# Expert rows weighted, gated and added straight into the residual's rows by the scatter, in a Trainium2 encoder layer

## The reference

```python
x = x + gt1 * token_mixer(h1)                     # attention half, not touched by the change
h = rms_norm(x, g_ffn) * (1.0 + sc2) + sh2
x = x + gt2 * hier_moe(h)                         # top-1 group, top-2 of its 8 experts
return rms_norm(x, g_final)

# hier_moe: 32 experts, each (silu(h @ w_gate) * (h @ w_up)) @ w_down, 1024 -> 512 -> 1024
# rows of a token's two experts are weighted by topw (k = 0, 1) and summed
out = jnp.einsum('nk,nkd->nd', topw, picked)
```

## Time and profile before

| what | value |
|---|---|
| median of three executions | 3067.68 us |
| the profiled execution | 3061.92 us |
| its span, first to last instruction | 3059.7 us |
| busy: PE, DVE, ACT, POOL | 2762.8, 1735.5, 1502.2, 817.3 us |
| mean granted TensorE clock | 0.954 |
| moved by DMA | 451.19 MB |
| router's last VectorE operations, about | 2014 to 2017 us |
| first and last `gate_up` start | 2031.47 and 2929.20 us |
| last scatter lands | 2968 us |

### The profile page before, as it was taken

How to read it: one execution, slowest core, us unless ns; L and a number is a source line. 1 busy time by engine, 2 the same in 40 slices (tenths; PEclk the granted TensorE clock), 3 DMA queues, 4 the chain that set the end, 5 groups by cost and what they waited for, 6 DMA issues and landing times.

```text
span 3059.7 us, 49933 instructions
## 1 busy us (share of the span) xinstructions
PE 2762.8 (90%) x14228; PEld 2320.1 (76%) x14229; DVE 1735.5 (57%) x3141; ACT 1502.2 (49%) x2615; POOL 817.3 (27%) x617
## 2 busy tenths in 40 slices
PE   8899999999999996899999799759999999999960
PEld 2399999999888875788888588647777787877740
DVE  3555655566667666545441244476765635375859
ACT  2455666667544443444432222246655634375744
POOL 1244444554322112244434111101111111111110
PEclk9999999999999998899999899869999999999985
DMA  7500000000000002443433344358976835486978
GB/s 263 202 24 25 27 23 25 25 24 25 22 19 16 10 11 64 133 138 129 138 121 113 137 165 161 128 196 309 345 273 249 302 144 219 140 329 235 366 285 339
DMA packets 195890, 451.19 MB, mean 147 GB/s; under 512 B 39959, under 2 KB 91159, under 8 KB 193773
## 3 DMA queue, kind: packets, MB, share of 16 engines
q1 hardware_dynamic: 176812, 389.46, 36.1%
q0 software_dynamic: 14400, 52.44, 4.5%
q10 hardware_dynamic: 4608, 8.39, 0.7%
HBM read 380.01 MB, written 70.21 MB: 147 GB/s over the span
## 4 chain that ended last, share of the span: by engine, by line
PE 72%; DVE 9%; issue 8%; DMA 6%; ACT 3%; DVEq 1%; POOL 1%; SPq 1%; ACTq 0%; POOLq 0%
PE bank L1672 14%; PE bank L1887 13%; PE bank L1771 5%; PE bank L1815 4%; DMA sb_w_in<-in_w_gate_up 3%; PE S_ps L1898 3%; PE E_ps L1898 3%; PE O_ps L1737 3%; PE S_ps L1771 3%; PE S_ps L1718 3%; PE E_ps L1771 3%; PE S_ps L1720 3%; PE bank L1638 2%; PE E_ps L1704 2%; PE S_ps L1815 1%
## 5 line engine op out<-in xcount | busy, mean ns | idle before, releaser
L1887 PE MATMUL bank<-sb_gu,sb_x_hiT 128*128 (+1 forms) x1568 | 500.5, 401 | 16.7 <-DVE sb_x_loT L1542 16.7
L724 POOL TENSOR_TENSOR sb_h_lo<-sb_hT,sb_h_hi 128x1024 fp32r<-128x1024 f32 x128 | 336.9, 2632 | 611.1 <-ACT sb_h_hi L839 611.1
L1672 PE MATMUL bank<-sb_w_hi,sb_h_hi 128*128 (+1 forms) x1024 | 402.0, 393 | 15.4 <-issue 9.0
L1887 PEld LDWEIGHTS bank<-sb_gu,sb_x_hiT 128*128 128x128 f32 x1568 | 297.7, 192 | 82.5 <-issue 17.7
L1672 PE MATMUL bank<-sb_w_hi,sb_h_lo 128*128 (+1 forms) x1024 | 344.7, 337 | 0.0
L1672 PE MATMUL bank<-sb_w_lo,sb_h_hi 128*128 (+1 forms) x1024 | 343.9, 336 | 0.0
L1528 DVE TENSOR_TENSOR sb_gu<-sb_w_in,sb_gu 128x1024 f32 (+1 forms) x256 | 303.4, 1223 | 60.0 <-ACT sb_gu L1069 55.7
L1069 ACT ACTIVATE sb_gu<-sb_w_in 128x1024 f32 (+1 forms) x256 | 262.8, 1057 | 129.5 <-DMA sb_w_in<-in_w_gate_up 114.8
L1887 PE MATMUL bank<-sb_gu,sb_x_loT 128*128 (+1 forms) x784 | 312.0, 398 | 0.0
L763 POOL TENSOR_TENSOR sb_g_lo<-sb_g_raw,sb_g_hi 128x1408 fp32r<-128x1408 f32 x64 | 212.5, 3341 | 338.1 <-ACT sb_g_hi L944 338.1
L1672 PEld LDWEIGHTS bank<-sb_w_hi,sb_h_hi 128*128 128x128 f32 x1024 | 193.9, 189 | 31.1 <-issue 19.1
(11 more groups left out here) (346 smaller groups left out, 6106.5 us busy)
## 6 DMA issues: line engine op xcount, KB each, us to landing
sb_w_in<-in_w_gate_up SPq DMA_DIRECT2D x256, 512.0 KB, 5.3
sb_w_in<-in_w_expert_down SPq DMA_DIRECT2D x128, 512.0 KB, 5.5
sb_g_raw<-in_w_gb SPq DMA_DIRECT2D x64, 704.0 KB, 4.1
sb_wada<-in_w_ada SPq DMA_DIRECT2D x24, 1024.0 KB, 7.7
sb_yp<-y_d SPq DMA_DIRECT2D x16, 1024.0 KB, 6.7
sb_w_raw<-in_w_qkv SPq DMA_DIRECT2D x128, 96.0 KB, 2.0
sb_x_round<-in_x SPq DMA_DIRECT2D x4, 2048.0 KB, 12.6
mT_d<-sb_mg ACTq DMA_DIRECT2D x32, 256.0 KB, 2.1
```

What stands on the lines that cost most here:

```text
L724: nc.gpsimd.tensor_tensor(h_lo[c][:], tile_src(g, T), h_hi[c][:].bitcast(F32), ALU.subtract).then_inc(sem("h_lo_ready"), 1)
L1672: last = nc.tensor.matmul(bank[c][:, 0:PASS_COLS].rearrange("p (a m) -> p a m", a=1), x[c][:, k, :], w[:, ds(row + k, 1), :], start=(k == ...
L1887: last = nc.tensor.matmul(PS[j][:].rearrange("p (a n) -> p a n", a=1), x[:, k, :], gu[:, ds(gu_row(e, part, k), 1), j * DE:(j + 1) * DE], ...
```

## The change

- The scatter adds (`compute_op=ALU.add`) the finished rows into `x1_d`, at the token's row. `x1_d` has 128 pad rows now, `h2_d` 128 instead of 64. One index table, `row_idx` = max(token, pair - 2048), serves both the gather and the scatter. `y_d` is gone.
- The rows are finished before the scatter: ScalarE's copy out of PSUM takes the pair's weight as its scale (`w_row`, one number per row), and VectorE multiplies by the gate (`gate_rows`), which stands in PSUM banks 6 and 7 (`GT2`). The hidden rows are therefore transposed into bank 2, with two new waits on TensorE.
- The weights of a block come by a new indirect gather (`weights_in`) from `w_d`, into which ScalarE stores `pair_w` once.
- In a block that opens an expert, ScalarE and VectorE convert pieces 0 to 3 (`EARLY`), then do the head of the block, then pieces 4 to 7 (`LATE`), then the tail. TensorE waits for the weights' low parts piece by piece.
- The last stage loads the sums in eight transfers of two tiles, all at once, into buffers of their own, and only squares, scales and stores. It is written out without loops.
- SP sends the gate's row and the pads (four of 256 KB, one of 512 bytes) where it sent three rows and one pad.

```diff
+                for n, (t, row) in enumerate(((gt1b, 2), (A2b, 4), (B2b, 3), (gt2b, 5))):
...
-                sp.dma_start(h2_d[SEQ:SEQ + PAD_ROWS // 2, :], zero_rows[:]).then_inc(sem("pads_out"), 16)
+                for pads in (h2_d, x1_d):
+                    for at in (SEQ, SEQ + PAD_ROWS // 2):
+                        sp.dma_start(pads[at:at + PAD_ROWS // 2, :], zero_rows[:]).then_inc(sem("pads_out"), 16)
+                sp.dma_start(w_d[2 * SEQ:2 * SEQ + PAD_ROWS, :].rearrange("(a n) b -> a (n b)", a=1), zero_rows[0:1, 0:PAD_ROWS]).then_inc(sem("pads_out"), 16)
...
+        sp.wait_ge(sem("experts_done"), 1)
+        for r in range(PAIRS):
+            sp.dma_start(acc[:, 2 * r:2 * r + 2, :], accv[:, 2 * r:2 * r + 2]).then_inc(sem(ACC_IN[r][0]), 16)
+        for t in range(TT):
             sp.wait_ge(sem("out_ready"), t + 1)
+            sp.dma_start(ov[:, t, :], acc[:, t, :]).then_inc(sem("out_stored"), 16)
...
         def scatter_block(g):
+            nc.gpsimd.tensor_copy(si, row_idx[:, ds(g, 1)]).then_inc(sem("si_ready"), 1)
             pool.wait_ge(sem("si_ready"), g + 1)
-            pool.wait_ge(sem("y_ready"), g + 2)
+            pool.wait_ge(sem("y_gated"), g + 1)
...
+            nc.gpsimd.indirect_dma_start(x1_d, bass.IndirectOffsetOnAxis(ap=si, axis=0), y_sb[:], None, compute_op=ALU.add).then_inc(sem("y_out"), 16)
+
+        def weights_in(g):
+
+            nc.gpsimd.tensor_copy(wi, scatter_idx[:, ds(g, 1)]).then_inc(sem("wi_ready"), 1)
+            pool.wait_ge(sem("wi_ready"), g + 1)
+            pool.sem_inc(sem("row_dmas"), 1)
+            nc.gpsimd.indirect_dma_start(w_row[:], None, w_d, bass.IndirectOffsetOnAxis(ap=wi, axis=0)).then_inc(sem("w_in"), 16)
...
         with pool.Fori(1, total) as g:
             pool.wait_ge(sem("xgT_done"), g + 2)
             gather_block(g + 2)
             scatter_block(g - 1)
+            weights_in(g)
             pool.wait_ge(sem("y_out"), 16 * g)
             pool.sem_inc(sem("y_free"), 1)
...
+        act.wait_ge(sem("rows_in"), 80)
+        act.wait_ge(sem("logits_ready"), TT)
+        for j in range(2):
+            last = nc.scalar.activation(GT2[j][:], gt2b[:, j * 512:(j + 1) * 512], ACT.Copy)
+        last.then_inc(sem("gt2_ready"), 1)
...
         def rows_out(g):
             act.wait_ge(sem("down_done"), g + 1)
             act.wait_ge(sem("y_free"), g + 1)
+            act.wait_ge(sem("w_in"), 16 * (g + 1))
             for j in range(2):
+                last = nc.scalar.activation(y_sb[:, j * 512:(j + 1) * 512], PS[4 + j][:], ACT.Copy, scale=w_row[:, 0:1])
...
+                    next_expert_high(g, e, EARLY)
+                    block_head(g)
+                    next_expert_high(g, e, LATE)
+                    block_tail(g)
                     down_high(g, e)
...
+        for r in range(PAIRS):
+            squares_of(2 * r)
+            squares_of(2 * r + 1)
+            if r > 0:
+                roots(r - 1)
+        roots(PAIRS - 1)
...
-        link(nc.vector.tensor_scalar(gather_idx[:], scatter_idx[:], 1, None, ALU.logical_shift_right))
+        link(nc.vector.tensor_scalar(token_i[:], scatter_idx[:], 1, None, ALU.logical_shift_right))
+        link(nc.vector.scalar_tensor_tensor(row_idx[:], scatter_idx[:], -float(SEQ), token_i[:], ALU.add, ALU.max))
...
+        def gate_rows(g):
+            dve.wait_ge(sem("y_ready"), g + 2)
+            for j in range(2):
+                cols = slice(j * 512, (j + 1) * 512)
+                last = nc.vector.tensor_tensor(y_sb[:, cols], y_sb[:, cols], GT2[j][:], ALU.mult)
+            last.then_inc(sem("y_gated"), 1)
+
+        def block_tail(g):
+            if not isinstance(g, int):
+                gate_rows(g - 1)
             dve.wait_ge(sem("hT_high"), g + 1)
...
+        def finish(r):
+            dve.wait_ge(sem("rms"), ROUNDS + TT + r + 1)
+            nc.vector.reciprocal(rstd3[:, 2 * r:2 * r + 2], rms3[:, 2 * r:2 * r + 2]).then_inc(sem("rstd"), 1)
+            dve.wait_ge(sem("rstd"), ROUNDS + TT + r + 1)
+            for t in (2 * r, 2 * r + 1):
+                nc.vector.scalar_tensor_tensor(acc[:, t, :], acc[:, t, :], rstd3[:, t:t + 1], gfb[:], ALU.mult, ALU.mult).then_inc(sem("out_ready"), 1)
...
         def gate_up(g, e):
             pe.wait_ge(sem("xT_ready"), g + 1)
-            pe.wait_ge(sem("gu_lo_ready"), KD * (e + 1))
             wait(pe, sem("h_ready"), g)
             for k in range(KD):
+                pe.wait_ge(sem("gu_lo_ready"), KD * e + k + 1)
...
         def turn_hidden(g):
             pe.wait_ge(sem("h_ready"), g + 1)
+            pe.wait_ge(sem("xT_ready"), g + 2)
             for k in range(KE):
-                last = nc.tensor.transpose(PS[6][:, k * P:(k + 1) * P], hg[:, k * P:(k + 1) * P], ident[:])
+                last = nc.tensor.transpose(PS[2][:, k * P:(k + 1) * P], hg[:, k * P:(k + 1) * P], ident[:])
...
+            turn_rows(g + 1, g)
```

More of the change, by code:

```diff
@@ L48 @@
 assert PIECES == 2 * RING
+EARLY, LATE = range(KD // 2), range(KD // 2, KD)
 MOD_CHUNKS = N_MOD * D // CHUNK
@@ L820, in _ @@
         gather_block(2)
+        pool.wait_ge(sem("w_out"), 16)
+        weights_in(0)
         with pool.Fori(1, total) as g:
@@ L1115, in _ @@
         act.wait_ge(sem("tables_ready"), 1)
+        act.dma_start(w_d[0:2 * SEQ, :].rearrange("(t p two) a -> p t (two a)", p=P, two=2), pair_w[:], allow_slow_non_contiguous=True).then_inc(sem("w_out"), 16)
         total = act.value_load(ends[0:1, E - 1:E], min_val=E, max_val=MAX_BLOCKS)
         rows_T(0)
-        next_expert_high(0, 0)
-        block(0)
+        block_head(0)
+        next_expert_high(0, 0, range(KD))
+        block_tail(0)
         down_high(0, 0)
@@ L1148, in last_round @@
-        def last_round(q, more):
-            for r in range(ROUND):
-                if r < ROUND - 1:
-                    weigh(q, r + 1)
-                elif more:
-                    weigh(q + 1, 0)
-                if r == 0 and not (isinstance(q, int) and q == 0):
-                    roots(q - 1)
-                t = ROUND * q + r
-                wait(act, sem("sumsq"), 2 * TT + t)
-                act.wait_ge(sem("acc_ready"), t + 1)
-                act.sem_inc(sem("last_waits"), 1)
-                nc.scalar.activation(sq3[:], acc_row(t), ACT.Square, accum_out=ssq3[:, r:r + 1]).then_inc(sem("sumsq"), 1)
@@ L1555, in _ @@
         total = dve.value_load(ends[0:1, E - 1:E], min_val=E, max_val=MAX_BLOCKS)
+        dve.wait_ge(sem("gt2_ready"), 1)
         rows_low(0)
-        next_expert_low(0)
-        block(0)
+        block_head(0)
+        next_expert_low(0, range(KD))
+        block_tail(0)
         down_low(0)
@@ L1564, in _ @@
                 with dve.If(e < E - 1):
-                    next_expert_low(e)
-            block(g)
-            with dve.If(e_was < e):
+                    next_expert_low(e, EARLY)
+                    block_head(g)
+                    next_expert_low(e, LATE)
+                with dve.Else():
+                    block_head(g)
+                block_tail(g)
                 down_low(e)
+            with dve.Else():
+                block_head(g)
+                block_tail(g)
+        gate_rows(total - 1)
@@ L1615, in _, with means @@
-        last_round(0)
-        last_round(1)
-        with dve.Fori(2, TT // ROUND) as q:
-            last_round(q)
-        finish(TT - LAG, ROUND - 1)
-        means(TT // ROUND - 1)
-        inverse_roots(TT // ROUND - 1)
-        for r in range(ROUND):
-            finish(TT - ROUND + r, r)
+        def means(r):
+            dve.wait_ge(sem("sumsq"), 2 * TT + 2 * r + 2)
+            nc.vector.tensor_scalar(ms3[:, 2 * r:2 * r + 2], ssq3[:, 2 * r:2 * r + 2], 1.0 / D, EPS, ALU.mult, ALU.add).then_inc(sem("meansq"), 1)
@@ new lines, in finish @@
+        def finish(r):
[4 more added lines that the diff above has]
+                nc.vector.scalar_tensor_tensor(acc[:, t, :], acc[:, t, :], rstd3[:, t:t + 1], gfb[:], ALU.mult, ALU.mult).then_inc(sem("out_ready"), 1)
+        means(0)
+        for r in range(PAIRS):
+            if r + 1 < PAIRS:
+                means(r + 1)
+            finish(r)
```

185 lines of the change are left out of this document (55 added, 130 removed).

## The result

The changed kernel takes 3050.25 us (median of 5 runs, 3042.10 to 3051.58) against 3066.09 for the kernel before beside it: a ratio of 0.994 (95% interval 0.9925 to 0.9955), 0.6% faster. The forecast was 3003, with 2984 to 3037 as its range. The sign was right, and about three quarters of the gain did not come. The profiled execution, the fastest of the five, took 3042.1 us, 19.8 less than the one before.

The account below looks back on a forecast made before the run. VectorE bounds the last stage; TensorE paces the expert stage, transfers limiting two stretches. Terms -45.1 - 24.2 + 1.1 + 3.5 + 0.3 = -64.4 from 3,061.9, plus 5.8, gave 3,003 us; range 2,984 to 3,037.

Parts of the forecast that it names:

- Last stage: Kernel's end: VectorE's limit goes, DMA limits at 396 GB/s, 46.5 us instead of 91.6; -45.1 (ends -38.4, -48.9).
- The rival of slow stores: Last stage: stores standing alone miss the mixed rate; at 342 GB/s it takes 53.2 us, total 3,010; chance 0.10.
- a chain through VectorE as a sign against me: Last stage: a chain running through ScalarE or VectorE would show the forecast wrong.
- The new order: Expert stage: Silu ahead of four pieces regains 20 of 24.4 us where unsaturated, and 5.5 us once per saturated stretch.
- The sign I had named: Expert stage: waits of L1905 for VectorE's product L1547 gone outside the two saturated stretches would show the forecast right.
- the expert stage's -24.2: Expert stage's total: 20 us regained in unsaturated stretches and -4.2 in the two saturated ones, adding scatter's cost included.
- a second pass of 1.38: Saturated stretches: the adding scatter also fetches its 512 KB, 1.38 us per block, making 20.5 us of DMA.
- Gating: Expert stage: two VectorE operations of 0.683 us per block, 18.8 us per opening block, below the DMA's 20.5.
- My first rival: The last stage gains, the expert stage does not, with VectorE and DMA near full; 3,027 or 3,034; chance 0.18.
- Middle and table: Before the experts: gate's row and pads ahead of output weights, +3.5 (ends 0, +6); one index operation, +0.3.
- End of the last block: Down projection starts earlier, -2.3; last gating +1.4 and slower scatter landing +2.0; sum +1.1 (ends -1, +7).
- The rival of the held buffer: Expert stage: scatter landing over 14.5 us holds y_sb and sets the pace; 3,146 at 18 us; chance 0.08.

Follow-up runs that it names:

- Run 4: The kernel before with only the new order of pieces, head and tail, and TensorE waiting piece by piece; 3033.1 us, ratio 0.989.
- run 11: The changed kernel with VectorE's gating moved behind the down conversions in blocks that open an expert; 3026.8 us, ratio 0.988.
- run 9: The changed kernel with padding dropped, gate's row loaded later, block 0 in old order, hidden transposes waiting for half, gating behind down conversions; 2994.1 us.
- run 6: The changed kernel with a plain scatter, no gating on VectorE, and the hidden rows' transposes in their own PSUM bank; 2992.2 us, ratio 0.975.
- run 1: The changed kernel with its scatter a plain write instead of an adding one; 3007.1 us, ratio 0.981.
- run 2: The changed kernel with all eight pieces ahead of the block's head again, scatter still adding; 3085.7 us, ratio 1.007.
- run 3: The changed kernel with all eight pieces ahead of the head and a plain scatter; 3058.2 us, ratio 0.998.
- run 7: The changed kernel with the scatter's pad rows dropped by a bound on the row's number; 3023.2 us, ratio 0.986.

## Why the prediction was wrong, point by point

- **Last stage**, -45.1: right in mechanism and nearly in size, -48.2. The rate was higher than any row I had: 410 and 420 GB/s in the two parts above. The rival of slow stores falls with that, since the second part is stores alone. The Trainium skill (DMA: Bandwidth & Descriptors, Specifications) gives about 358 GB/s of HBM for one core; this trace does not agree, with 387 over the stage. I had named a chain through VectorE as a sign against me; it is there (L1587), at a DMA share of 1.02, so it tells nothing.
- **The new order**: right. Run 4 against the kernel before: -22.5 in the other 37 steps (forecast -20) and -10.8 in the nine full ones (5.5 us of relief in each stretch made -11; the sum's own end without the second pass, -16.4, was too far, since it also took the DMA's work in a step, 19.2, for the step's length, 19.6). The sign I had named holds: in the changed kernel L1877, the line that was L1905, has no wait for VectorE's product.
- **The adding scatter** is the main step that failed, in the expert stage's -24.2, which came as +16.3. Price: 2.1 us of the engines a block, where I took a second pass of 1.38. In the nine full steps that is a question of size only, 14.6 us (193.0 - 178.4) against 9 x 1.38 = 12.4. What was wrong is where I counted it. I gave it nothing elsewhere, because the DMA share there was 0.74. But 0.74 is a mean over steps that open an expert and steps that don't. An opening block needs more of the engines than a step's 17.82 us in any stretch: 19.2 by my sum, and still 18.7 in run 4, at a share of 1.00. As I read it, the six buffered ring pieces and the quiet steps around it carry it through, and with the adding they no longer do. The cost is where opening blocks stand together: each of the three pairs takes 19.5 to 19.8 us in its second step instead of 17.8, and where three and four of them follow each other 7.1 and 5.6 us are lost. Cost in the other 37 steps: 685.0 - 663.9 = 21.1 us. The Trainium skill (DMA: Bandwidth & Descriptors, Rules for kernel authors) says that an accumulating DMA reads its destination and writes it later. Packets of twice the time agree with that, though no record shows the reading itself.
- **Gating** costed at nothing beside the DMA: wrong by 11.2 us. I had VectorE at 18.8 us of work in an opening block (17.5 in the trace) against 20.5 of the DMA, and took the larger for the limit. But the two are not side by side: in an opening block the down conversions that free ring buffers stand behind the gating, so its 1.4 us are added to the load that waits for them. Moved behind them it gives 1.3 and 1.6 us a step back (runs 11 and 9). My first rival came near ("ring slots come free later since four pieces wait for the head"), but its 3,027 to 3,034 let the stage lose 6.8 us at most.
- **A wait that I did not see**: I priced the new wait of the next rows' transposes, but not that of the hidden rows' transposes for the next rows in the bank they now share: 47.5 us of waiting in all, some 3.3 us of it in the steps, by one execution.
- **The stage's opening** was not in the sum. Block 0's own pieces now stand behind its head: 4.3 us in run 4 (36.0 to 40.3), 6.2 in the changed kernel. The old order for that one block brings it to 35.0.
- **Middle and table**, +3.8: +4.9 in the profiled run, near by luck. First gate/up lies between +3.6 and +11.5 in the eight kernels that share this part (2035.0 to 2043.0), and most of that spread is there before the output projection, which the change doesn't touch. Followed by the same matmuls of TensorE, from 1725 to 1750 us in the kernel before, the middle costs 5.7 us (5.2 to 5.8 in the eight; -0.8 to +1.4 in the four with the row behind the weights and no pads). That is inside my end of +6, but not by my path: the wo_raw step of the chain is shorter (6.22 us, was 8.86) and starts later, because the five issues of pads hold SP's queue for 7.0 us, where that end had 0.56 each. The new index operation takes 0.23.

```profile
1734.52 3.79 SPq L588 DMA_DIRECT2D h_d<-sb_zero_rows  x2
1738.35 2.66 SPq L588 DMA_DIRECT2D x_d<-sb_zero_rows  x2
...
1741.54 6.22 DMA sb_wo_raw<-in_w_out
```

- **End of the last block**, +1.1: +1.2, by another path. The weights' gather stands behind the scatter before it, and the last rows wait for it:

```profile
2977.78 2.39 POOL x_d L790
...
2981.77 5.22 DMA sb_w_row<-w_d,sb_picks
...
2987.59 0.69 ACT sb_y_sb L1091
2988.31 1.30 DVE sb_y_sb L1539 x2
...
2990.42 6.23 DMA x_d<-sb_y_sb,sb_picks
```

- **The rival of the held buffer** falls: the landing of 10.3 us is under the 14.5 that it needed, and no copy into the buffer waits for a scatter.

The expert stage in one line: 861.7 - 33.3 (order) - 0.6 (weights and their gather, run 6 against run 4) + 3.3 (bank) + 11.2 (gating) + 35.7 (adding) = 878.0. The terms hang together: the adding is 23.6 in the old order, and with the adding in place the gating's move alone gives 21.9 (run 11).

## What to carry to other kernels

A mean share of 0.74 is no room: take the shared resource's work per kind of step, and compare it with the length of that step. Where transfers and conversions hand buffers to each other round a ring, look for the operations that stand in series there: they add, as the gating did, also where each engine is under the step's length alone. When a stage gains from fewer bytes, ask what the bytes cost where they went, and drop padding before paying for it twice.

## What the runs showed of the hardware

- An adding scatter's 4096-byte packets take 328 ns (median of the last block) against 159 for a plain one. Its landing is 10.3 us against 7.0 in run 1, and 6.4 against 4.1 in the old order (runs 2 and 3).
- Rows dropped by the bound still leave a packet each (15968 in run 7 as in the changed kernel), of 8 bytes and 9 ns by the records.
- A DMA share of 0.99 is not by itself a limit: 21.4 us a step at 0.99 in the changed kernel, 20.1 at 1.01 in run 11, with the same transfers. So the share times the step, 21.2 and 20.3 us, is no fixed amount of work.
- Stores alone reached 420 GB/s for 16 us.
